# Input tokens of the later stages at a pitch of 256 columns, on multiples of 1024 bytes

## What is computed

```python
# layer 1, on 16 + 256 tokens; the output keeps the last 256
u = rms_norm(h, norm_mix_pre)
a, g = split(u @ conv_w_in + conv_b_in)            # first projection, 272 tokens
u = a * sigmoid(g)
u = silu(layer_norm(causal_depthwise_conv31(u)))
h = h + rms_norm(u @ conv_w_out + b, norm_mix_post)
u = rms_norm(h, norm_ffn_pre)
h = h + rms_norm((silu(u @ w_gate) * (u @ w_up)) @ w_down, norm_ffn_post)
# layer 2, on the 256 tokens
p = rms_norm(x, norm1) @ w_in_2                     # q, k, v, forget gates, pooled input, branch gates
y = gates[0] * (forgetting_attention(q, k, v) @ w_a) + gates[1] * (multiscale_pool(pin) @ w_p)
x = x + y @ w_out_2
x = x + peer(rms_norm(x, norm2))                    # 8 heads pick 16 of 16384 experts for each token
```

## Time and profile before

| | |
|---|---|
| median of 3 runs | 2957.41 us (2955.88 to 2958.62) |
| the profiled execution | 2961.6 us |
| its span, first to last instruction | 2959.4 us |
| TensorE matmuls busy | 2748.9 us, 93% of the span |
| VectorE, ScalarE, GpSimd busy | 64%, 44%, 22% |
| DMA, mean over the span | 267 GB/s |

### The profile page before, as it was taken

How to read it: one execution, slowest core, us unless ns; L and a number is a source line. 1 busy time by engine, 2 the same in 40 slices (tenths; PEclk the granted TensorE clock), 3 DMA queues, 4 the chain that set the end, 5 groups by cost and what they waited for, 6 DMA issues and landing times.

```text
span 2959.4 us, 47035 instructions
## 1 busy us (share of the span) xinstructions
PE 2748.9 (93%) x18175; PEld 2078.1 (70%) x18175; DVE 1881.6 (64%) x3067; ACT 1296.6 (44%) x2473; POOL 663.6 (22%) x576
## 2 busy tenths in 40 slices
PE   8999899999999998999999999999998878888885
PEld 8996788888888887989999889677764432222221
DVE  7885566565565565455445558888858874555556
ACT  5555443333333344435334345555566532233223
POOL 0000000000000000040000002444447675555554
PEclk9999999999999998999999999999996679999997
DMA  6443545555555553443555656999999999999998
GB/s 257 176 166 127 199 174 189 192 184 185 189 193 184 186 190 124 157 147 141 183 185 184 241 199 243 372 408 417 412 385 411 405 407 423 422 422 419 419 419 347
DMA packets 132598, 790.37 MB, mean 267 GB/s; under 512 B 34774, under 2 KB 34774, under 8 KB 37142
## 3 DMA queue, kind: packets, MB, share of 16 engines
q1 hardware_dynamic: 55040, 393.16, 35.9%
q0 software_dynamic: 77008, 394.46, 33.0%
q10 hardware_dynamic: 384, 0.52, 0.1%
HBM read 944.95 MB, written 4.19 MB: 321 GB/s over the span
## 4 chain that ended last, share of the span: by engine, by line
PE 65%; DMA 17%; DVE 10%; issue 4%; ACT 2%; POOL 2%; POOLq 0%; DVEq 0%; ACTq 0%
PE bank L2073 12%; PE bank L2074 12%; PE bank L2075 12%; DMA s_u<-in_expert_u,s_u_index 11%; PE bank L2079 10%; PE bank L2515 5%; DMA s_v<-in_expert_v,s_v_index 5%; PE bank L2080 5%; DVE s_u L1933 3%; PE bank L2570 3%; PE bank L2525 2%; DVE s_w_lo L1306 1%; POOL s_u L658 1%; DVE s_yrow L1614 1%; PE bank L2171 1%
## 5 line engine op out<-in xcount | busy, mean ns | idle before, releaser
L1306 DVE TENSOR_TENSOR s_w_lo<-s_raw,s_w_hi 128x2048 fp32r<-128x2048 f32 x288 | 661.3, 2296 | 597.0 <-ACT s_w_hi L705 592.9
L705 ACT ACTIVATE s_w_hi<-s_raw 128x2048 fp32r<-128x2048 f32 x284 | 543.9, 1915 | 805.6 <-PE bank L2075 530.0
L2079 PE MATMUL bank<-s_a,s_w_hi 128*128 128x512 f32 x1408 | 495.0, 394 | 3.2 <-DVE s_w_lo L1306 3.2
L2073 PE MATMUL bank<-s_a,s_w_hi 128*128 128x256 f32 (+1 forms) x1632 | 465.5, 285 | 3.4 <-DVE s_a L1330 1.8
L2075 PE MATMUL bank<-s_a,s_w_lo 128*128 128x256 f32 (+1 forms) x1632 | 463.1, 284 | 0.0
L2074 PE MATMUL bank<-s_a,s_w_hi 128*128 128x256 f32 (+1 forms) x1632 | 462.7, 284 | 0.0
L1933 DVE CUSTOM_DVE_ANT_0 s_u<-s_u,s_xn_late 128x1024 f32<-128x1024 f32 x256 | 304.0, 1225 | 223.7 <-DMA s_u<-in_expert_u,s_u_index 197.3
L2570 PE MATMUL bank<-s_v,s_spread 128*32 128x512 f32 x2048 | 309.0, 715 | 139.3 <-DMA s_v<-in_expert_v,s_v_index 107.0
L2080 PE MATMUL bank<-s_a,s_w_lo 128*128 128x256 f32 x1408 | 395.3, 281 | 0.0
L658 POOL DMA_INDIRECT s_u<-in_expert_u,s_u_index x256 | 297.4, 1162 | 359.9 <-DVE s_halfdot L1933 207.3
L678 POOL DMA_INDIRECT s_v<-in_expert_v,s_v_index x256 | 311.5, 1217 | 231.0 <-PE bank L2570 140.3
(11 more groups left out here) (352 smaller groups left out, 3397.4 us busy)
## 6 DMA issues: line engine op xcount, KB each, us to landing
s_raw<-in_stream SPq DMA_DIRECT2D x292, 1024.0 KB, 4.8
s_raw<-in_expert_v SPq DMA_DIRECT2D x40, 1024.0 KB
s_raw<-in_dense_u SPq DMA_DIRECT2D x37, 1024.0 KB
s_tap_blocks<-in_taps POOLq DMA_DIRECT2D x9, 512.0 KB, 3.5
s_u<-in_expert_u,s_u_index POOLq DMA_INDIRECT x256
s_v<-in_expert_v,s_v_index POOLq DMA_INDIRECT x256
s_panel_early<-in_dense_u POOLq DMA_DIRECT2D x3, 1024.0 KB, 10.8
s_xres<-in_x SPq DMA_DIRECT2D x2, 1024.0 KB, 6.0
```

Of the source, the lines that this page charges most:

```text
L705: act.activation(w_hi[s % 2][:, :], raw[s][:, :], ACT.Copy).then_inc(hi_ready, 1)
L1306: dve.tensor_tensor(w_lo[s % 2][:, :], raw[s][:, :], w_hi[s % 2][:, :].bitcast(f32), ALU.subtract)\
L2073: pe.matmul(dst, left[0], right[0], start=start, stop=False)
L2079: pe.matmul(dst, left[0], both, start=start, stop=False)
```

## The change

s_a gets a pitch of 256 columns (T) instead of 272 (L): each half and each block begins on a multiple of 1024 bytes. The first projection keeps the old layout, as a tile s_a_in of its own name at the same place; the two tiles share memory, since no stage uses both. S does not move, so the end of the old tile, 2048 bytes in each partition, is not covered by the new s_a. This strip is a tile s_a_rest, and GpSimd clears it with a memset ahead of the row loads for the FFN. s_xnt gets the pitch of 256 too, at the same start.

```diff
-    a_both = keep("s_a", [128, 2, KT, L], f32r)
+    A = at
+    a_in = keep("s_a_in", [128, 2, KT, L], f32r)
+    a_both = place("s_a", [128, 2, KT, T], A, f32r)
     a_hi, a_lo = a_both[:, 0], a_both[:, 1]
     S = at
+    a_rest = place("s_a_rest", [128, (S - A) // 4 - 2 * KT * T], A + 2 * KT * T * 4)
...
-    xnt = place("s_xnt", [128, KT, L], ring0 + 64 * K)
+    xnt = place("s_xnt", [128, KT, T], A)
...
             pool.wait_ge(panel_used, 1 + 32 + 6)
+            step(pool.memset(a_rest[:, :], 0.0))
             pool.dma_start(gffn_row[:, :], g_ffn_post.partition_broadcast(128)).then_inc(rows_loaded, 16)
...
-                act.activation(a_hi[:, four, :], a_f[:, four, :], ACT.Copy).then_inc(a_hi_ready, 1)
+                act.activation(a_in[:, 0, four, :], a_f[:, four, :], ACT.Copy).then_inc(a_hi_ready, 1)
...
-                    dve.tensor_tensor(a_lo[:, four, :], a_f[:, four, :], a_hi[:, four, :].bitcast(f32), ALU.subtract).then_inc(a_lo_ready, 1)
+                    dve.tensor_tensor(a_in[:, 1, four, :], a_f[:, four, :], a_in[:, 0, four, :].bitcast(f32), ALU.subtract).then_inc(a_lo_ready, 1)
...
-                                ins = product(bank[p][:, 0:L], (w_hi[s][:, where], w_lo[s][:, where]), (a_hi[:, k, :], a_lo[:, k, :]),
+                                ins = product(bank[p][:, 0:L], (w_hi[s][:, where], w_lo[s][:, where]), (a_in[:, 0, k, :], a_in[:, 1, k, :]),
                                               start, stop)
```

## The result

| | before | after |
|---|---|---|
| median | 2957.93 us (22 runs, 2955.76 to 2961.65) | 2963.74 us (22 runs, 2961.13 to 2968.37) |
| ratio after/before, 95% interval | | 1.0019 (1.0013 to 1.0025) |
| profiled execution, span | 2961.6 us, 2959.4 us | 2962.36 us, 2960.6 us |
| first dense-expert matmul on s_xnt (TensorE, from the span's start) | 1836.91 us | 1842.31 us |

The changed kernel takes 5.8 us more, 0.19%: within the range of the forecast and within the 0.2%, but with an interval that lies wholly above 1, and on the other side of the 2.0 us that the sum had gained. The two profiled spans differ by only 1.2 us because the part from the first dense-expert matmul on varies between executions: it took 1122.5 us in the profile of before and 1118.3 us in that of after, and 1118.2 to 1123.2 us in all fourteen profiles of this case.

The account below looks back on a forecast made before the run. TensorE's steps were taken to bound the part up to about 1830 us, DMAs the rest; +5.5 - 4.5 - 3.0 = -2.0 us on 2957.4 us gave 2955.4 us, range 2946 to 2966 us.

Parts of the forecast that it names:

- What bounds the kernel: TensorE's matmul steps set the time up to about 1830 us; the gathered experts behind wait on DMAs.
- (a): Triples with 256 moving columns, 3456 matmuls: step from 118.4 to 119.95 ns, 5.5 us lost.
- (b): Token-major stages, 912 matmuls of 512 columns with s_a as weights: 231.7 to 226.8 ns, 4.5 us gained.
- (c): FFN gate and up, 1408 pairs of a long and a short matmul: 349.1 to 346.7 ns, 3.0 us gained.
- sign of being wrong: FFN gate and up: the prediction is wrong if a pair moves by over 4 ns either way.
- the jump between pieces: In the pairs' long matmul, going from high-half to low-half piece costs nothing visible: 230.7 ns against 231.7 ns for one piece.
- The first slower rival: FFN pairs: long-short alternation settles on the long side; 2972.5 us, deciding from 352.6 ns a pair; chance 0.18.
- The give-back of one panel in eight: Each FFN round's second panel waits 0.31 us; a faster first panel lengthens that, so 7/8 of the pairs' gain counts.
- (d): First projection unchanged; dense-expert matmuls on s_xnt taken as nothing, with 1.9 us either way left to the range.
- (e): VectorE and ScalarE write the same elements with the same instruction counts: nothing.
- (f): The strip's memset on the GpSimd queue takes 0 to 1.8 us; 54 us cover it, nothing on the path.
- The third rival: The layout does nothing: apparent alignment effects come from the stages themselves, tokens' steps stay; 2957.4 us, chance 0.12.

Follow-up runs that it names:

- long and short apart: Changed kernel, but in each bank of the FFN's gate and up panels all eight long matmuls run first, then the eight short ones; 2957.94 us, ratio 1.0001.
- side by side: Changed kernel, but for the FFN's gate and up the two halves of each block are neighbours, so the long matmul reads one 512-column run; 2962.93 us, ratio 1.0014.

## Why the prediction was wrong, point by point

**What bounds the kernel: right.** TensorE's steps set the part ahead of the dense experts; each term that was measured shows in the start of the first dense-expert matmul.

**(a) and (b): right.** 120.0 ns and 226.7 ns against the 119.95 and 226.8 ns taken from aligned neighbours, +5.4 and -4.3 us against +5.5 and -4.5. These stages run one kind of step without a break, and in the kernel with long and short apart each kind so run settles on these values: that an aligned row of the same form is a good price for such a run is borne out at this start.

**(c): the step that failed.** It took the pair for the sum of two settled steps, 226.8 + 119.95 = 346.7 ns. That sum exists: the first round has it, and so do four of the later ones with the halves side by side; but its parts in the first round are 230 and 117 ns, so the working doesn't explain it, and whether the agreement is more than luck isn't shown. An alternation of long and short has a second level, 353.3 ns, on the same addresses, and the changed kernel runs at it in ten rounds of eleven: 4.2 ns over before, beyond the 4 ns that the prediction had set as a sign of being wrong. The term was forecast at -3.0 us and measured +4.2 us; this 7.2 us is nearly all of the miss of 7.8 us between the forecast gain of 2.0 us and the 5.8 us lost. What misled me was the reasoning that the jump between pieces costs nothing "that I can see" and that the rest is alignment. The first half is right (side by side, the values are the same); the second left out that a step depends on the steps around it. I also read the spread in the earlier trace rows as a sign of position. The changed kernel's pairs spread as far, 232 to 241 and 114 to 120 ns, with every token at the same start: such a spread doesn't tell position from sequence, and no single step is the price of its kind.

**The first slower rival came true in kind.** It said that the alternation settles on the long side and decides from 352.6 ns a pair; 353.3 ns was measured. It had the mechanism, and its price of 2972.5 us was the bound, not the size: the long step settles at 232 to 241 ns and the short at 114 to 120 ns, +4 ns a pair and not +10. I gave it 0.18 because the aligned 512-column step was the fastest of its class, which is true and says nothing of the alternation.

**The give-back of one panel in eight: right, with the sign turned.** I said that a faster first panel lengthens the 0.31 us wait. It became slower, 352.7 for 347.6 ns a pair, 0.08 us in all, and the wait became shorter by as much: from a later round's start to its second panel's first matmul it is 6.04 us before and after.

**(d), (e), (f): right.** The first projection has 126.1 ns a step in both profiles. The dense-expert matmuls on s_xnt, for which 1.9 us were left to the range, keep 215.8 ns a step at the old pitch and at all four starts. The memset takes 0.53 us, inside the 0 to 1.8 us (the second row load is issued 0.49 us later, not 1 to 2), and its cover of over 50 us holds.

**The third rival, that the layout does nothing: refuted.** Starts 64 bytes apart move the triples between 113.4 and 120.0 ns. TensorE: Matmul & The Clock Gate, section "Back-to-back issue gap", of the Trainium skill gives an isolated step by the number of columns, by which an estimate for 256 is 109.2 ns, and has no term for the address; the traces have 113.4 to 120.0 ns by the start alone, and the measurement decides.

**What stays open.** What meets inside the chip, why 192 bytes is the best start for the triples, and why the later rounds of the changed kernel enter the slow sequence while its first round enters the other: the runs show that a wait or one swapped pair can change the sequence, not what about them does. In the triples the load of the next weights starts some 3 ns behind each matmul and is printed as 192 ns at 0 bytes and as 187 or 188 ns at 192 bytes; that loads and moving tokens hinder each other is a suspicion that no run here tests. All weights lay on multiples of 512 bytes in every kernel; moving them in place of the tokens wasn't tried.

## What to carry to other kernels

A step is the price of a sequence, not of an instruction: a row of the same form and start in a uniform stretch priced another uniform stretch to 0.1 ns here, but the sum of two such rows doesn't price their alternation. Where tokens all start at one place, that place is a parameter to be timed for each kind of matmul, and the roundest address need not be best: 192 bytes past a multiple of 256 took 5.5% off the aligned 256-column step here. When a loop's iterations on the same addresses differ in time by a few tenths of a microsecond, read the single steps in a fast and a slow iteration before looking for a wait.

## What was not expected of the hardware

- The step of a matmul depends on where its operands start, by 64 bytes: 113.4, 117.8, 118.7 or 120.0 ns for 256 moving columns at 192, 64, 128 or 0 bytes past a multiple of 256, and 226.9 to 233.3 ns for 512 columns with the tokens as weights. The granted clock was 1.00 in the stretches read. The fp32 matmuls on s_xnt, 256 columns too, have 215.8 ns at all four.
- A step depends on its neighbours' operands: moving the low half by 64 bytes changed also the two matmuls of a triple that don't read it, from 120.0 to 118.9 and 118.0 ns.
- An alternation of two kinds has more than one sequence on which it stays: 346.7 and 353.3 ns with both halves at 0, 346.7 and 349.9 ns with the low half at 64. A wait or one swapped pair can switch it, and what follows keeps it to the end of the round.
